# A two-block transformer kernel on one core: the second block's attention values in row form, and the softmax's transposes moved behind units of weights

## The reference, cut to what matters

```python
def hybrid_layer(x, w_in, ...):
    proj = x @ w_in
    aq, ak, av, ag, bq, bk, bv, bg, cu, cglu, cg = jnp.split(proj, IN_OFFSETS, axis=-1)
    ...
    ya = diff_attention(...aq, ak, av...)      # 4 heads of 128, two softmaxes a head, a = p0 - lam * p1
    ya = ya * jax.nn.silu(ag)
    yb = dilated_attention(...bq, bk, bv...)   # 8 heads of 128
    yb = yb * jax.nn.silu(bg)
    yc = conformer_conv(cu, cglu, ...)         # gated, 31 taps, layer norm, swish, pointwise w_pw
    yc = yc * jax.nn.silu(cg)
    y = jnp.concatenate([ya, yb, yc], axis=-1) @ w_out
    return layer_norm(ALPHA * x + y, ln_g, ln_b)
```

## Time and profile before

| | |
|---|---|
| median of 3 runs | 2909.24 us (2908.48 to 2909.68) |
| profiled execution | 2909.73 us |
| its span, first to last instruction | 2907.9 us |
| granted TensorE clock, mean | 1.000 |
| PE, PEld busy | 2886.8 us, 2497.7 us |
| DVE, ACT, POOL busy | 2071.9 us, 1362.5 us, 418.9 us |
| DMA | 520.58 MB, mean 179 GB/s |

### The profile page before, as it was taken

One profiled execution on the slowest core, in us unless ns is written; L12 is line 12 of the kernel. 1 busy time (PEld: TensorE's weight loads), 2 busy tenths in 40 slices (PEclk: granted clock), 3 DMA queues, 4 the chain that ended last, 5 costly groups with the idle time before them and its releaser, 6 DMA issues.

```text
span 2907.9 us, 43426 instructions
## 1 busy us (share of the span) xinstructions
PE 2886.8 (99%) x16142; PEld 2497.7 (86%) x16142; DVE 2071.9 (71%) x2314; ACT 1362.5 (47%) x1618; POOL 418.9 (14%) x392
## 2 busy tenths in 40 slices
PE   9999999999999999999999999999999999999999
PEld 7888888888888888888888888888888888888887
DVE  6666667875786676766666667876887856788766
ACT  6554544346654444443343344544344545444453
POOL 1000001104010000000000000013950100891010
PEclk9999999999999999999999999999999999999999
DMA  6555556654466666656555665556555554555455
GB/s 218 175 172 166 168 188 188 208 160 133 134 196 191 186 198 196 198 187 192 175 182 180 195 195 182 178 191 193 169 174 160 159 194 153 175 174 173 158 176 174
DMA packets 479573, 520.58 MB, mean 179 GB/s; under 512 B 17720, under 2 KB 438699, under 8 KB 479176
## 3 DMA queue, kind: packets, MB, share of 16 engines
q1 hardware_dynamic: 474528, 509.68, 55.7%
q0 software_dynamic: 4080, 6.30, 0.8%
q10 hardware_dynamic: 824, 2.69, 0.3%
HBM read 516.49 MB, written 2.12 MB: 178 GB/s over the span
## 4 chain that ended last, share of the span: by engine, by line
PE 64%; DVE 6%; ACT 2%; issue 1%; DMA 0%; DVEq 0%; POOL 0%; ACTq 0%; POOLq 0%
PE PG L2108 37%; PE PG L2111 18%; DVE WL L1268 2%; PE PG L2140 2%; PE PG L2142 2%; PE PG L2141 2%; ACT WH L650 1%; DVE G L1281 1%; DVE MIX L1704 0%; PE PX L2172 0%; PE PX L2225 0%; PE PX L2161 0%; PE PX L2324 0%; PE PX L2333 0%; DVE G L1587 0%
## 5 line engine op out<-in xcount | busy, mean ns | idle before, releaser
L1268 DVE TENSOR_TENSOR WL<-RAW,WH 128x1024 fp32r<-128x1024 f32 (+1 forms) x956 | 1150.5, 1232 | 499.8 <-ACT WH L650 486.2
L650 ACT ACTIVATE WH<-RAW 128x1024 fp32r<-128x1024 f32 (+1 forms) x972 | 997.5, 1050 | 785.2 <-PE PG L2111 451.4
L2108 PE MATMUL PG<-XH,WH 128*128 128x512 f32 x4096 | 1294.9, 397 | 6.6 <-DVE XH L1952 3.2
L2111 PEld LDWEIGHTS PG<-XH,WL 128*128 128x128 f32 x4096 | 769.4, 188 | 181.8
L2111 PE MATMUL PG<-XH,WL 128*128 128x256 f32 x4096 | 805.0, 278 | 0.0
L2108 PE MATMUL PG<-YH,WH 128*128 128x512 f32 x2336 | 736.3, 396 | 2.0 <-DVE WL L1268 1.9
L2108 PEld LDWEIGHTS PG<-XH,WH 128*128 128x128 f32 x4096 | 625.2, 189 | 13.8 <-issue 7.7
L2111 PEld LDWEIGHTS PG<-YH,WL 128*128 128x128 f32 x2336 | 438.8, 188 | 103.7
L2111 PE MATMUL PG<-YH,WL 128*128 128x256 f32 x2336 | 459.0, 278 | 0.0
L2108 PEld LDWEIGHTS PG<-YH,WH 128*128 128x128 f32 x2336 | 355.9, 189 | 5.9 <-issue 3.4
L1281 DVE TENSOR_REDUCE G<-PG 128x512 f32<-128x1024 f32 x174 | 212.0, 1219 | 33.9 <-PE PG L2111 33.8
(11 more groups left out here) (302 smaller groups left out, 2092.0 us busy)
## 6 DMA issues: line engine op xcount, KB each, us to landing
RAW<-in_w_in_dram SPq DMA_DIRECT2D x488, 512.0 KB, 4.6
RAW<-in_w_ffn_gu_dram SPq DMA_DIRECT2D x176, 512.0 KB, 4.6
RAW<-in_w_ffn_down_dram SPq DMA_DIRECT2D x88, 512.0 KB, 4.6
RAW<-in_w_out_dram SPq DMA_DIRECT2D x64, 512.0 KB, 4.6
RAW<-in_w_rnn_out_dram SPq DMA_DIRECT2D x40, 512.0 KB, 4.5
RAW<-in_w_attn_out_dram SPq DMA_DIRECT2D x32, 512.0 KB, 4.7
RAW<-in_w_o_dram SPq DMA_DIRECT2D x32, 512.0 KB, 4.7
RAW<-in_w_ple_gate_dram SPq DMA_DIRECT2D x32, 512.0 KB, 4.9
```

The lines of the kernel that those rows point to most:

```text
L650: nc.scalar.activation(WH[:, u % SLOTS, 0:nk, :], RAW[:, u % SLOTS, 0:nk, :], ACT.Copy)\
L1268: V_.tensor_tensor(WL[:, u % SLOTS, 0:nk, :], RAW[:, u % SLOTS, 0:nk, :], WH[:, u % SLOTS, 0:nk, :].bitcast(fp), ALU.subtract).then_inc(s. ...
L2108: mm(PG[:, 2 * par + j, :], WH[:, slot, kk, P * j:P * j + P], x, start=grp.opens and n == 0 and kk == 0, stop=False)
L2111: last = mm(PG[:, 2 * par + j, T:2 * T], WL[:, slot, kk, P * j:P * j + P], x[:, 0:T], start=False, stop=grp.closes and n == len(units) - 1 ...
```

## The change

The values of the second block are computed in row form, so that they need no transposes: a wide group of 512 columns gives the values of four heads at once, and DVE copies it from PSUM to V (`values`). The value groups of a layer are now three wide ones of eight units: two in `dil`, each for two turns, one in `diffa` for all four differential heads; `diffb` has none. `dil` is written out without a loop. `take` and `give` split a group's units in parts, so that jobs stand between them: the first units of the next group are split ahead of a job. The scores, transposes and output products are hung behind a unit inside a group (`in_dil`, `in_diffa`, `z_diffb`), and the transposes of the last softmax behind the sixth unit of `outa`.

```diff
-        V = F[:, 2048:2560].rearrange("p (a n) -> p a n", a=4)
+        V = AL[:, 20 * 2 * T:22 * 2 * T].rearrange("p (b n) -> p b n", b=NB)
...
+            dil = []
+            for i in range(2):
+                a, b = ([Group(w2, DC, B0 + 1024 * o + COLS * pair_, 0, XH) for o in (0, 1, 3)]
+                        for pair_ in (2 * i, 2 * i + 1))
+                v = Group(w2, DC, B0 + 2048 + 2 * COLS * i, 0, XH, wide=True)
+                dil += [a[0], a[1], v, a[2]] + b
+            phases.append(Phase(f"dil{l}", 1, dil))
+            phases.append(Phase(f"diffa{l}", 1, [part(0, 0), part(1, 0), part(2, 0, wide=True), part(3, 0)]))
+            phases.append(Phase(f"diffb{l}", 1, [part(0, 1), pw[0], part(1, 1), pw[1], part(3, 1, pool=range(4))],
+                                {1: [6]}))
...
             def transposed():
                 dve.wait_ge(s.turned, c.next("turned"))
-                V_.tensor_copy(V, PX[:, 2, :].rearrange("p (a n) -> p a n", a=4))
                 V_.tensor_copy(PTS, PX[:, 0:2, 0:384]).then_inc(s.ready, 1)
                 dve.wait_ge(s.ready, c.next("ready"))
 
-            def gate(grp, tell=False):
+            def values(grp):
+
+                par = c.n.get("group", 0) % 2
+                dve.wait_ge(s.unit, c.next("seen", grp.seen))
+                V_.tensor_copy(V, PG[:, 2 * par:2 * par + 2, :]).then_inc(s.evac, 1)
...
+            def take(grp, n):
+                split(grp, slice(ahead[0], n))
+                ahead[0] = 0
+
+            def give(grp, n):
+                split(grp, slice(0, n))
+                ahead[0] = n
...
+                for i in range(2):
+                    q0, k0, v, g0, q1, k1, g1 = body[7 * i:7 * i + 7]
+                    take(q0, 4)
+                    if i:
+                        gate(body[6])
+                        give(k0, 2)
+                        transposed()
+                        taps(7, 1, l)
+                    else:
+                        for job in before:
+                            job()
+                    take(k0, 4)
+                    evacuate(q0, two(QR[:, 0, :]))
+                    taps(8 * i, 1, l)
+                    give(v, 2)
+                    if i:
+                        dil_out(1)
+                    take(v, 4)
+                    evacuate(k0, two(QR[:, 1, :]))
+                    taps(8 * i + 1, 2, l)
+                    split(v, slice(4, 8))
+                    dil_softmax(2 * i)
+                    take(g0, 4)
+                    values(v)
+                    transposed()
+                    take(q1, 4)
+                    gate(g0)
+                    dil_out(2 * i)
+                    taps(8 * i + 3, 1, l)
+                    take(k1, 4)
+                    evacuate(q1, two(QR[:, 0, :]))
+                    taps(8 * i + 4, 1, l)
+                    take(g1, 4)
+                    evacuate(k1, two(QR[:, 1, :]))
+                    taps(8 * i + 5, 2, l)
+                    give(body[7] if i == 0 else following, 2)
+                    dil_softmax(2 * i + 1)
...
                     if j == 1:
                         c.add("act")
                     else:
-                        split_next(f"diffb{l}", 5, 1)
                         diff_out(0, l)
+                        give([p for p in phases if p.name == f"outa{l}"][0].body[0], 2)
+                        diff_softmax(1, l)
...
-            def heads_out(tell):
+            def heads_out(half):
                 ready()
                 for h in range(2):
-                    o = T * h
-                    mm(PX[:, 3, o:o + T], V[:, 2 * h, :], W[:, h, 0:T], start=True, stop=False)
-                    last = mm(PX[:, 3, o + P:o + T], V[:, 2 * h + 1, :], W[:, h, T:T + P], start=False, stop=True)
-                last.then_inc(tell, 1)
+                    o, at = T * h, P * (2 * half + h)
+                    mm(PX[:, 3, o:o + T], V[:, 0, at:at + P], W[:, h, 0:T], start=True, stop=False)
+                    last = mm(PX[:, 3, o + P:o + T], V[:, 1, at:at + P], W[:, h, T:T + P], start=False, stop=True)
+                last.then_inc(s.heads2, 1)
...
+            def in_dil(n):
+
+                i, what = divmod(n, 7)
+                return {0: {2: lambda: pt_soft(1)} if i else None,
+                        1: {2: lambda: heads_out(1)} if i else None,
+                        2: {3: z_dil, 7: lambda: pt_soft(1)},
+                        3: {3: lambda: heads_out(0)},
+                        6: {2: z_dil}}.get(what)
...
+                return ({2: lambda: pt_soft(1)}, {2: conv_sums}, {1: conv_squares, 4: z_diffa},
+                        {1: lambda: pt_soft(2)})[n]
+
+            def z_diffb():
                 pe.wait_ge(s.evac, c.value("group", -1))
+                pe.wait_ge(s.op, c.value("op", 2))
+                z_soft(2)
...
+                        elif ph.name[:5] == "diffb" and j == 4:
+                            mid = {1: z_diffb}
...
-                                mid = {0: diff_sum, 1: lambda: turn_x(0)} if j == 1 else None
+                                mid = ({5: lambda: pt_soft(2)}, {0: diff_sum, 1: lambda: turn_x(0)}, None, None)[j]
```

More of the change, by code:

```diff
@@ new lines, in diffa_gate @@
+            def diffa_gate():
+                silu_gate()
+                from_dve()
+                nc.scalar.activation(SC_SQ, CA, ACT.Tanh, scale=0.5).then_inc(s.act, 1)
+                act.wait_ge(s.act, c.next("act"))
+                from_dve()
+                for q in range(2):
+                    nc.scalar.activation(hi2(YH, q, base=DC), CA[:, 2 * q:2 * q + 2, :], ACT.Copy, scale=0.5)\
+                        .then_inc(s.act, 1)
+                    act.wait_ge(s.act, c.next("act"))
@@ new lines, in give, with dil_softmax @@
+            def give(grp, n):
+                split(grp, slice(0, n))
+                ahead[0] = n
+            def dil_softmax(pair_):
+                dve.wait_ge(s.scores2, c.next("scores2"))
+                scores(2, QSCALE, lambda x: 2 * pair_ + (4 + x))
+                inverse_sums(2)
+                for h in range(2):
+                    for b, (lo, up) in enumerate(((0, P), (P, 3 * P))):
+                        x = S4[:, h, lo:up]
+                        ins = V_.tensor_scalar(x, x, der(D_RED + 16 + 2 * h + b), None, ALU.mult)
+                ins.then_inc(s.ready, 1)
+                dve.wait_ge(s.ready, c.next("ready"))
@@ L2332, in pt_soft @@
                     for to, frm in ((0, 0), (P, P), (2 * P, 2 * P)):
-                        nc.tensor.transpose(PX[:, h, to:to + P], x[:, frm:frm + P], IDENT)
-                v_transposes(c.n["group"] % 2).then_inc(s.turned, 1)
+                        last = nc.tensor.transpose(PX[:, h, to:to + P], x[:, frm:frm + P], IDENT)
+                last.then_inc(s.turned, 1)
             def diff_sum():
@@ new lines, in z_dil, with conv_sums @@
+            def z_dil():
+                pe.wait_ge(s.evac, c.value("group"))
+                z_soft(1)
+            def in_dil(n):
[5 more added lines that the diff above has]
+                        6: {2: z_dil}}.get(what)
+            def conv_sums():
+                heads_out(1)
+                pe.wait_ge(s.conv, c.next("conv"))
+                for ch in range(CONVC):
+                    last = sum_features(0, CA[:, ch, :], ch == 0, ch == CONVC - 1)
+                last.then_inc(s.sum, 1)
@@ new lines, in conv_squares, with z_diffa, in_diffa @@
+            def conv_squares():
+                squares_in()
+                for ch in range(CONVC):
+                    last = sum_features(1, SC_SQ[:, ch, :], ch == 0, ch == CONVC - 1)
+                last.then_inc(s.sumsq, 1)
+            def z_diffa():
+                pe.wait_ge(s.evac, c.value("group"))
+                ready()
+                z_soft(2)
+            def in_diffa(n):
+                return ({2: lambda: pt_soft(1)}, {2: conv_sums}, {1: conv_squares, 4: z_diffa},
+                        {1: lambda: pt_soft(2)})[n]
@@ L2387, in after_outa @@
             def after_outa(i, j, l):
                 if j == 0:
-                    heads_out(s.heads2)
+                    heads_out(1)
                 if j == 2:
```

286 lines of the change are left out of this document (136 added, 150 removed).

## The result

Six runs of the changed kernel gave a median of 2920.07 us (2918.96 to 2922.07), six of the kernel before 2909.59 (2908.48 to 2910.59). The ratio is 1.0037, its 95% interval 1.0024 to 1.0049: the change costs 10.5 us. That lies above the forecast range and on the side that had a chance of 0.17.

A forecast was written before the change was run, and what follows sets the result against it. The prediction took PE, busy 99% of the span, as the bound. On 2909.7 us its terms, -5.3 - 3.1 - 5.2 + 11.8 + 0.2 + 2.4, summed to +0.8, giving 2910 as the median, range 2901 to 2917.

The forecast's parts named there:

- the side that had a chance of 0.17: Slower by over 0.2%: the dilated stage turns DVE-bound while POOL computes, 2916.5 us, plus a little upper tail; chance 0.17.
- old wait in `dil`: Second half of the dilated stage: a weight unit starting 0.86 us after the matmuls before it; 1.7 us saved, both layers.
- old wait before the first differential softmax's transposes: Transposes of the first differential softmax start 1.16 us after the last matmul pair, 0.23 being normal; 1.8 us saved.
- small convolution's last unit: Last unit of the small convolution, about half a microsecond late for DVE; the wait goes, 0.8 us saved.
- stretch of the moved value group: The stretch that held the moved value group: PE waits less for DVE, 0.9 us saved for two layers.
- wait at the third unit of `outa`: Third output unit after pw[1]: PE waits for DVE's chain, stretched by POOL; 5.9 us a layer, 11.8 in all.
- scores of the second differential softmax: In `diffb`: the scores wait for DVE's second subtraction, 0.1 us a layer, 0.2 added.
- output product behind its transposes: Second differential softmax: transposes directly ahead of the output product, PE waits for DVE's copy; 1.2 us a layer, 2.4 added.
- the walk: Step-by-step timing of the new order with the old trace's durations; second differential softmax starts at E + 13.5, E ending pw[1].
- DVE is ahead at the first of these: Second half of the dilated stage: DVE no longer late at the weight unit that started after 0.86 us; 1.7 us saved.
- The rival of a DVE-bound stage: Dilated stage, DVE stretched by POOL: fifth value unit of the second half 2.4 us late, 2916.5 us; chance 0.17.
- this mechanism: The forecast's own case: PE and DVE savings offset by new waits at the second differential softmax, 2910 us; chance 0.45.

## Why the prediction was wrong

The terms, in us for both layers; "measured" is the distance from start to start less the normal one, or the count times the rows' distance.

| term | forecast | measured |
|---|---|---|
| 48 transposes of the values | -5.3 | -5.3 (in `dil` ten in 1.01, now six in 0.57) |
| 48 units in row form | -3.1 | -3.2 (2.787 to 2.720) |
| old wait in `dil` | -1.7 | +1.8 |
| old wait before the first differential softmax's transposes | -1.8 | -1.1 |
| small convolution's last unit | -0.8 | -1.0 |
| stretch of the moved value group | -0.9 | -0.3 |
| wait at the third unit of `outa` | +11.8 | +12.5 |
| scores of the second differential softmax | +0.2 | +0.2 |
| output product behind its transposes | +2.4 | +2.6 |
| low clock | none | +5.1 |
| sum | +0.8 | +11.3 |

The two profiled spans differ by 10.6. The 0.7 us the other way lie mostly at the differential softmaxes: there the ten matmuls took 1.35 us three times of four in the kernel before, and the six of the first one take 0.63 now.

The mechanism of the forecast was right and so were its two large prices. The contention of POOL with DVE carried the sum: without it 2.4 us a layer were forecast and 2.43 measured, with it 5.9 and 6.2. The softmax began at 13.1 us after the end of pw[1] (2306.64) where the walk said 13.5. That it came so close is partly luck: the walk had 4.6 us of stretching with 0.6 of it hidden behind the wait for POOL, measured were 3.9 with nothing hidden. The split behind waits 0.43 us for ACT's high part, with POOL's work small as well, because ACT makes it behind the high part of YH that the chain itself delivers.

Two steps failed, and it took both to leave the range, whose top is 2917: without the 5.1 us of the first the result would have been 2915.0, without the 3.5 of the second 2916.6. The first is the sum's silence on the clock, a missing term. The prediction priced a wait of 6 us on PE at 6 us. In the kernel before, every granted clock in the rows is 1.00, and PE's longest wait in the block is 1.8 us, so no row of it shows what a long wait costs afterwards; that should have been a bound on the upper side, and the range should have reached further up. The low clock cost 5.1 us by the trace, and filling the wait gave back 4.7 to 5.4.

The second is "DVE is ahead at the first of these" in the part on what leaves DVE. That walk of the dilated stage used a split at its undisturbed 1.2 us, though the same prediction held that DVE stands still beside POOL and though the earlier trace rows had DVE 10% busier where POOL computes. The trace of the kernel before had the stretch in plain sight, four splits beside POOL's taps in 5.81 us against the 4.63 of the earlier trace rows, where POOL is idle:

```profile
2115.23 5.81 DVE L1268 TENSOR_TENSOR WL<-RAW,WH 128x1024 fp32r<-128x1024 f32 x4 [0.51 <-ACT WH L650]
```

The prediction used 1.4 us a split only in its rival. With pairs at 2.9 to 3.3 instead of 2.36, DVE is late at two units a layer. Instead of 1.7 saved, 1.8 were lost: 3.5 us. With the taps made small the late units went; so did they with one split moved into DVE's idle time. The rival of a DVE-bound stage named the right cause and the wrong place: it expected the fifth value unit 2.4 us late, but the late ones are the third units of the next turn's first two groups, and DVE still has idle time between them.

The small terms were off by a microsecond together: the transposes after the first differential softmax are still 0.39 us late in each layer (0.3 in the text, but then counted as gone), and the 0.9 of the moved group was mostly not there.

The chances put 0.45 on this mechanism with a result near no change. It was the right case with two costs left out, 8.6 us together.

## What to carry to other kernels

A wait on PE can have two prices, its length and the low clock behind it: here waits of 6.2 and of 2.4 us had both, in both layers. Where a change makes such a wait, the second price is added as a range (1.3 to 2.8 us behind each of these), or the wait is filled. Where two engines contend, the stretched duration belongs in every stage in which both work, not only in the one where a row shows it in full. And an engine that is late can still be idle just ahead: here one split moved between a softmax's scores and its sums took two late units away, and with the other moves of this kind a loss of 10.5 us became a gain of 10.4.

## What was not expected of the hardware

A gap of 2.66 us on PE, from start to start, was followed by a granted clock of 0.50 in both layers. The gap of 2.1 us at the start of the second layer, which every kernel here has, was followed by it in the profiled execution of the changed kernel and in none of the other eleven. It may differ by execution: of the kernel with the splits inside the softmax, six executions at a mean clock of 1.000 took 2902.4 to 2903.4 us and five at 0.999 took 2904.4 to 2904.9. Behind which gap those five have it no profile shows, and what decides it stays open.
